# Differential attention's scores on all 128 rows of TensorE: stacked queries, doubled keys, key rests beside zeros

## The reference, cut to what matters

```python
q = (h @ w_q).reshape(b, nb, Q_BLOCK, N_HEADS, 2, HEAD_DIM)        # HEAD_DIM = 64
logits = einsum('bqhmd,bkhmd->bhmqk', q, k) * HEAD_DIM ** -0.5     # m: the two maps
logits = where(dist >= 0, logits + bias, -inf)
probs = softmax(logits)
attn = probs[:, :, 0] - lam * probs[:, :, 1]
o = einsum('bhqk,bkhe->bqhe', attn, v)
```

## Time and profile before

| | us |
|---|---|
| median of 3 runs | 1964.98 (1963.58 to 1965.52) |
| span of the profiled execution | 1962.9 |
| PE busy, share of the span | 1940.2, 99% |
| DVE, ACT, POOL busy | 1248.2, 827.2, 319.8 |
| granted TensorE clock, mean | 0.997 |

### The profile page before, as it was taken

How to read it: one execution, slowest core, us unless ns; L and a number is a source line. 1 busy time by engine, 2 the same in 40 slices (tenths; PEclk the granted TensorE clock), 3 DMA queues, 4 the chain that set the end, 5 groups by cost and what they waited for, 6 DMA issues and landing times.

```text
span 1962.9 us, 27288 instructions
## 1 busy us (share of the span) xinstructions
PE 1940.2 (99%) x10578; PEld 1675.1 (85%) x10578; DVE 1248.2 (64%) x2219; ACT 827.2 (42%) x1377; POOL 319.8 (16%) x257
## 2 busy tenths in 40 slices
PE   9999999999999999999999999999999999999997
PEld 8998888888888988898888889887888888888897
DVE  7676666267775754388777525786673877774256
ACT  5233333244565532344444334465554444442343
POOL 2332332101241100201111010120112011110102
PEclk9999999999999999999999999999999999999998
DMA  5323222222212235322232322232112222233221
GB/s 173 104 76 100 87 81 91 92 86 94 69 44 76 78 99 137 108 90 93 86 107 98 119 88 84 83 122 78 44 55 86 87 86 96 98 109 117 96 66 64
DMA packets 54839, 179.02 MB, mean 91 GB/s; under 512 B 6167, under 2 KB 10775, under 8 KB 54712
## 3 DMA queue, kind: packets, MB, share of 16 engines
q1 hardware_dynamic: 54712, 177.29, 28.8%
HBM read 172.55 MB, written 4.72 MB: 90 GB/s over the span
## 4 chain that ended last, share of the span: by engine, by line
PE 93%; DVE 4%; ACT 1%; issue 1%; POOL 0%; DMA 0%; SPq 0%; DVEq 0%; ACTq 0%; POOLq 0%
PE pb L829 88%; PE pb L2737 1%; PE pb L932 1%; DVE WL L810 1%; PE pb L916 1%; DVE FR L1048 0%; PE pb L1767 0%; PE pb L2782 0%; DVE X L1013 0%; PE pb L920 0%; PE pb L1414 0%; DVE FR L903 0%; ACT WH L799 0%; DVE FD L1004 0%; DVE T L3011 0%
## 5 line engine op out<-in xcount | busy, mean ns | idle before, releaser
L829 PE MATMUL pb<-FR,WH 128*128 128x512 f32 (+1 forms) x5100 | 1443.2, 369 | 6.2 <-DVE FR L1048 3.2
L829 PEld LDWEIGHTS pb<-FR,WH 128*128 128x128 f32 x5100 | 914.5, 189 | 163.5 <-issue 5.9
L829 PE MATMUL pb<-FR,WL 128*128 128x512 f32 (+1 forms) x2550 | 934.9, 367 | 0.0
L810 DVE TENSOR_TENSOR WL<-stage,WH 128x1024 fp32r<-128x1024 f32 (+1 forms) x311 | 401.5, 1308 | 403.2 <-ACT WH L799 402.1
L829 PEld LDWEIGHTS pb<-FR,WL 128*128 128x128 f32 x2550 | 480.7, 189 | 79.6
L799 ACT ACTIVATE WH<-stage 128x1024 fp32r<-128x1024 f32 (+1 forms) x311 | 319.8, 1051 | 115.1 <-PE pb L829 108.6
L829 PE MATMUL pb<-WH,FR 128*128 128x256 f32 x832 | 155.9, 285 | 0.4 <-DVE WL L810 0.4
L829 PEld LDWEIGHTS pb<-WH,FR 128*128 128x128 f32 x832 | 131.6, 192 | 1.2 <-DVE WL L810 0.8
L1291 POOL TENSOR_TENSOR acc<-acc,T 128x512 f32<-128x512 f32 (+1 forms) x52 | 64.1, 1233 | 408.8 <-ACT T L1262 273.9
L829 PEld LDWEIGHTS pb<-FR 128*128 128x128 f32 x752 | 109.3, 190 | 10.8 <-issue 2.6
L829 PE MATMUL pb<-WL,FR 128*128 128x256 f32 x416 | 117.7, 283 | 0.0
(11 more groups left out here) (237 smaller groups left out, 1654.2 us busy)
## 6 DMA issues: line engine op xcount, KB each, us to landing
stage<-in_ws SPq DMA_DIRECT2D x310, 512.0 KB, 3.6
scr<-FD SPq DMA_DIRECT2D x16, 160.0 KB
X<-in_xT SPq DMA_DIRECT2D x8, 256.0 KB, 6.4
FD<-in_decay SPq DMA_DIRECT2D x8, 256.0 KB, 3.9
FD<-scr SPq DMA_DIRECT2D x1, 2048.0 KB, 8.5
out_dram<-X SPq DMA_DIRECT2D x16, 128.0 KB, 1.7
FD<-in_rope_b SPq DMA_DIRECT2D x2, 512.0 KB, 3.6
FD<-in_pT SPq DMA_DIRECT2D x4, 256.0 KB, 4.9
```

The lines of the kernel that those rows point to most:

```text
L810: dve.tensor_tensor(lo, src, hi.bitcast(F32), ALU.subtract).then_inc(*self.tick("w_lo", ("w_lo", u)))
L829: m = pe.matmul(out, l, r, start=first and i == 0, stop=last and i == n - 1)
```

## The change

A head's queries take 1024 columns as before, but now 512 columns for each map, on all 128 partitions: hi of the map on its own 64 partitions and the rest on the other 64. The keys' buffer grows from 1024 to 2048 columns: for each map, hi of the keys on both halves (512 columns), and the rest of the keys on the map's own half with zeros on the other half (512 columns). One matmul of 128 rows of stacked queries against doubled keys gives hi*hi and lo*hi in one, and a second against rest-and-zeros gives hi*lo. So a block of scores has four matmuls of 128 rows in place of six of 64.

```diff
-        self.dif_k = [fr(D0 + 4096 + 1024 * i, 1024) for i in range(2)]
+        self.dif_k = [fr(o, 2048) for o in (D0 + 4096, D0 + 10240)]
...
+    def dif_half(self, p):
+
+        return slice(64 * p, 64 * p + 64), slice(64 - 64 * p, 128 - 64 * p)
+
+    def dif_q(self, h, p):
+        return self.dif_qz[:, 1024 * h + 512 * p:1024 * h + 512 * p + 512]
...
         def scores(h, i):                                   # PE
-                for w in (("q_lo", h), ("dif_k", h)):
+                for w in (("q_lo", h), ("k_lo", h), ("k_twice", h)):
...
-            for a, b in ((0, 0), (0, 1), (1, 0)):
-                for p in range(2):
-                    hs, o = slice(64 * p, 64 * p + 64), 1024 * h + 512 * a + 128 * i
-                    m = pe.matmul(self.place["dif", "s", h, i, p][:, 0:n], QZ[hs, o:o + 128],
-                                  K[hs, 512 * b:512 * b + n], start=(a, b) == (0, 0), stop=a == 1)
-                    if a == 1:
-                        m.then_inc(*self.tick("pe_scores", ("pe", "dif", "s", h, i, p)))
+                o = 1024 * h + 512 * p + 128 * i
+                q, both, rest = QZ[:, o:o + 128], K[:, 512 * p:512 * p + n], K[:, 1024 + 512 * p:1024 + 512 * p + n]
+                self.mm(pe, self.place["dif", "s", h, i, p][:, 0:n], [(q, rest), (q, both)]).then_inc(
+                    *self.tick("pe_scores", ("pe", "dif", "s", h, i, p)))
...
         def query(h):                                       # ACT
-            act.activation(QZ[:, 1024 * h:1024 * h + 512], self.place["t", "dif", "q", h], ACT.Copy).then_inc(
-                *self.tick("q_hi", ("q_hi", h)))
+            for p in range(2):
+                rows = slice(0, P) if p == 0 and h >= 4 else self.dif_half(p)[0]
+                act.activation(self.dif_q(h, p)[rows, :], t[rows, :], ACT.Copy).then_inc(
+                    *self.tick("q_hi", ("q_hi", h, p)))
+
+        def query_rest(h):                                  # ACT, heads 4 to 7
+            act.wait_ge(*self.at("q_rest", h))
+            for p in range(2):
+                own, other = self.dif_half(p)
+                act.activation(self.dif_q(h, p)[other, :], self.place[t][own, :], ACT.Copy)
...
         def key(h):                                         # ACT
-            if h >= 3:
-                rounded(h - 3)
             if h % 2 == 0:
                 self.hi_to(act, BLOCK["w_kv_2", KD - 1, h])
-                if h:
-                    self.hi_to(act, BLOCK["w_kv_2", 3, 9 + h])
...
-            act.activation(self.dif_k[h % 2][:, 0:512], self.place["t", "dif", "k", h], ACT.Copy).then_inc(
-                *self.tick("k_hi", ("k_hi", h)))
+            for p in range(2):
+                own, _ = self.dif_half(p)
+                act.activation(K[own, 512 * p:512 * p + 512], self.place["t", "dif", "k", h][own, :],
+                               ACT.Copy).then_inc(*self.tick("k_hi", ("k_hi", h, p)))
+            if h and h % 2 == 0:
+                self.hi_to(act, BLOCK["w_kv_2", 3, 9 + h])
+            if h >= 3:
+                rounded(h - 3)
+            act.wait_ge(*self.at("k_hi", h, 1))
+            for p in range(2):
+                own, other = self.dif_half(p)
+                k = K[:, 512 * p:512 * p + 512]
+                act.activation(k[other, :], k[own, :].bitcast(F32), ACT.Copy).then_inc(
+                    *self.tick("k_twice", ("k_twice", h)))
...
-        for h in range(6):                                  # ACT's order
+        for h in range(2):
             query(h)
         self.hi_to(act, BLOCK["w_q_2", KD - 1, 7])
+        for h in range(2, 5):
+            query(h)
         query(6)
         query(7)
         key(0)
         self.hi_to(act, BLOCK["w_kv_2", KD - 1, 9])
+        query(5)
         value(0, [0])
...
             if h < 7:
                 scores(h, 1)
+                if h == 0:
+                    query_rest(4)
+                    query_rest(5)
...
             turn(h, 1)
             if h < 7:
                 c = (h + 1) // 2
+                if h == 0:
+                    query_rest(6)
+                    query_rest(7)
                 value(c, [(h + 1) % 2])
...
+        def query_rest(h):                                  # DVE, heads 0 to 3
+            dve.wait_ge(*self.at("q_hi", h, 1))
+            for p in range(2):
+                own, other = self.dif_half(p)
+                q = self.dif_q(h, p)
+                dve.tensor_tensor(q[other, :], self.place[t][own, :], q[own, :].bitcast(F32), ALU.subtract)
...
         def key(h):                                         # DVE
-            if h % 2 == 0:
+            if h == 0:
                 self.lo_to(dve, BLOCK["w_kv_2", KD - 1, h])
...
+            if h and h % 2 == 0:                            # behind the scaling, L2992
+                self.lo_to(dve, BLOCK["w_kv_2", KD - 1, h])
...
         for h in range(6):                                  # DVE's order
             query(h)
+        query_rest(0)
         self.lo_to(dve, BLOCK["w_q_2", KD - 1, 7])
         query(6)
         query(7)
+        query_rest(1)
         key(0)
+        query_rest(2)
         self.lo_to(dve, BLOCK["w_kv_2", KD - 1, 9])
+        query_rest(3)
         value(0, [0])
...
         def key(h):                                         # POOL
-            pool.wait_ge(*self.at("k_hi", h))
-            pool.tensor_tensor(o[:, 512:1024], self.place[t], o[:, 0:512].bitcast(F32), ALU.subtract)
+            for p in range(2):
+                own, _ = self.dif_half(p)
+                pool.wait_ge(*self.at("k_hi", h, p))
+                if p:
+                    pool.wait_ge(*self.at("k_lo first", h))
+                pool.tensor_tensor(K[own, 1024 + 512 * p:1536 + 512 * p], self.place[t][own, :],
+                                   K[own, 512 * p:512 * p + 512].bitcast(F32), ALU.subtract)
+            pool.wait_ge(*self.at("k_lo", h))
...
+        def zeros(h, after):
+            pool.memset(self.dif_k[h][:, 1024:2048].bitcast(F32), 0.0)
...
+        zeros(0, ("pe", "ffn0", "o", 7))                    # POOL's order
+        query(4)
+        zeros(1, ("pe", "dif", "q", 7))
+        query(6)
+        query(7)
         key(0)
+        query(5)
```

More of the change, by code:

```diff
@@ L2851, in query @@
         def query(h):
+            t = self.place["t", "dif", "q", h]
             act.wait_ge(*self.at("q_in", h))
-            act.activation(QZ[:, 1024 * h:1024 * h + 512], self.place["t", "dif", "q", h], ACT.Copy).then_inc(
-                *self.tick("q_hi", ("q_hi", h)))
+            for p in range(2):
[3 more added lines that the diff above has]
+        def query_rest(h):
+            t = ("t", "dif", "q", h)
+            act.wait_ge(*self.at("q_rest", h))
+            for p in range(2):
+                own, other = self.dif_half(p)
+                act.activation(self.dif_q(h, p)[other, :], self.place[t][own, :], ACT.Copy).then_inc(
+                    *self.tick("q_shifted", ("q_lo", h), ("free", *t)))
         def key(h):
-            if h >= 3:
-                rounded(h - 3)
+            K = self.dif_k[h % 2]
             if h % 2 == 0:
                 self.hi_to(act, BLOCK["w_kv_2", KD - 1, h])
-                if h:
-                    self.hi_to(act, BLOCK["w_kv_2", 3, 9 + h])
             act.wait_ge(*self.at("dif_kin", h))
@@ L2983, in query @@
                 *self.tick("q_in", ("q_in", h), ("free", *b)))
+        def query_rest(h):
+            t = ("t", "dif", "q", h)
+            dve.wait_ge(*self.at("q_hi", h, 1))
+            for p in range(2):
+                own, other = self.dif_half(p)
+                q = self.dif_q(h, p)
+                dve.tensor_tensor(q[other, :], self.place[t][own, :], q[own, :].bitcast(F32), ALU.subtract).then_inc(
+                    *self.tick("q_rest", ("q_lo", h), ("free", *t)))
         def key(h):
-            if h % 2 == 0:
+            if h == 0:
                 self.lo_to(dve, BLOCK["w_kv_2", KD - 1, h])
@@ L3159, in key @@
         def key(h):
-            t, o = ("t", "dif", "k", h), self.dif_k[h % 2]
-            pool.wait_ge(*self.at("k_hi", h))
-            pool.tensor_tensor(o[:, 512:1024], self.place[t], o[:, 0:512].bitcast(F32), ALU.subtract).then_inc(
-                *self.tick("k_lo", ("dif_k", h), ("free", *t)))
+            t, K = ("t", "dif", "k", h), self.dif_k[h % 2]
+            if h < 2:
+                pool.wait_ge(*self.at("k_zeros", h))
+            for p in range(2):
[4 more added lines that the diff above has]
+                pool.tensor_tensor(K[own, 1024 + 512 * p:1536 + 512 * p], self.place[t][own, :],
+                                   K[own, 512 * p:512 * p + 512].bitcast(F32), ALU.subtract).then_inc(
+                    *self.tick("k_lo", *([("k_lo", h), ("free", *t)] if p else [("k_lo first", h)])))
+            pool.wait_ge(*self.at("k_lo", h))
+        def zeros(h, after):
+            pool.wait_ge(*self.at(*after))
```

(15 more changed lines are left out.)

## The result

| | before | after |
|---|---|---|
| time, median | 1964.88 us (1963.58 to 1966.81, 6 runs) | 1972.16 us (1970.68 to 1974.0, 6 runs) |
| ratio to before | | 1.0037, interval 1.0027 to 1.0047 |
| span of the profiled execution | 1962.9 us | 1970.3 us |

The change costs 7.3 us, 0.37%. The forecast was 3.0 us slower, and 1972.16 lies just above its range, 1960.5 to 1972.

A forecast was written before the change was run, and what follows sets the result against it. PE, busy 99% of the span, was taken as the bound, with ACT and DVE pacing odd heads. Terms -2.7 + 2.4 + 2.3 + 1.0 = +3.0 us gave 1968.0 us on the median; range 1960.5 to 1972.

The forecast's parts named there:

- PE's saving kept: Cheaper score blocks on PE, kept only in blocks 1 to 3 of heads 0, 2, 4 and 6: -2.7 us.
- POOL's hold in heads 3 and 5: POOL's key-rest subtractions delay DVE's L3031 ahead of the combine by 1.2 us in each head: +2.4 us.
- the entry, first bias: Before the first values, extra ACT copies and DVE query rests make the first bias late: +2.3 us.
- ACT's chain in head 0: Four ACT copies for query_rest(6) and (7) ahead of head 0's values make these late into head 1: +1.0 us.
- PE's blocks: Four full matmuls a block: 0.91 us from block 3's start to the next matmul, PE saving 0.87 us a head.
- PE to wait at scores(4,1): At scores(4,1), start of head 4, PE's wait was to grow from 0.42 us to nearly 2 us.
- The clearing: POOL's clearing of 1024 columns in front of query(6): from nothing to 2.6 us, taken as 1.3 us.
- Rival D: Entry jams as rests alternate with POOL: +4 us, 1.5 more for a clearing; +6 to +7, so 1971.5; chance 0.14.
- rival A: The forecast itself, summed over entry and heads: +3.0 us, from +0.5 to +5.5 by the bounds; chance 0.50.
- Rival E: Full score blocks on PE aren't cheaper, 0.65 us more a head: +8 us, 1973; chance 0.04.

The follow-up runs named there:

- experiment 1: Kernel before with only PE's scores changed to four 128-row matmuls a block over the old buffers, output not the reference's: 1963.9 us, 0.9994.
- experiment 2: Changed kernel with ACT's rounded copy of an older head put back ahead of the key, as before the change: 1968.47 us, 1.0019.
- experiment 3: Changed kernel with DVE's query rests 2 and 3 moved from the entry to behind the biases of scores(0,1) and scores(0,2): 1970.87 us, 1.003.
- experiment 9: experiment 6 with ACT's two doubling copies of key 1 in head 0 moved behind the exponentials of scores(0,3): 1964.74 us, 0.9998.
- experiment 4: Changed kernel with matmuls nobody reads filling PE's waits ahead of scores(0,1), turn(3,2) and turn(5,2): 1968.99 us, 1.0022.
- experiment 5: Changed kernel with the moves of experiment 2 and experiment 3 together: 1966.42 us, 1.0006.
- experiment 6: experiment 5 with the rest of query 7 made by DVE in head 0, ahead of its values, instead of by POOL and ACT: 1966.2 us, 1.0004.
- experiment 11: Changed kernel with all its ACT, DVE and POOL work, but three pairs of 64-row matmuls for each block of scores: 1973.93 us, 1.0049.

## Why the prediction missed

The forecast was +3.0 us, and the profiled execution after is 7.26 us late. By its own terms:

| term | forecast | measured | from |
|---|---|---|---|
| PE's saving kept | -2.7 | -1.70 alone; -2.45 as the remainder | experiment 1; 7.53 less the four lines below |
| POOL's hold in heads 3 and 5 | +2.4 | +1.95 | after against experiment 2 |
| the entry, first bias | +2.3 | +3.70 | after; experiment 3 |
| ACT's chain in head 0 | +1.0 | +1.07 | (0,3) to (1,0); experiment 9 |
| TensorE's low clock behind the waits | none | +3.26 | after against experiment 4 |
| behind the stage | none | -0.27 | 7.53 at its end, 7.26 at the end of the span |

- **PE's blocks cost what was forecast** (0.91 us for scores(0,3)), and the saving is kept in even heads only. Its amount there was put too high: 0.67 us for a head, and 0.4 to 0.5 came through in experiment 1. I had counted block 1, which in heads 2, 4 and 6 stands behind a wait and saves next to nothing. The remainder of the sum gives 2.45, but this number carries the errors of all other lines; in experiment 5, where no hold and no low clock is left, it is 1.80 (1.08 less 1.82 and 1.06).
- **POOL and DVE meet in heads 3 and 5** as forecast, and experiment 2 shows that it is the place of one copy on ACT that makes them meet. The Trainium skill ("SBUF — State Buffer", Who interferes with whom) says that a DVE instruction with two SBUF inputs contends with a GpSimd instruction that reads SBUF; L3075 at 1.70 us beside POOL's subtraction and at 0.62 without it agrees. I had expected PE to wait at scores(4,1). The wait came earlier, 1.67 us ahead of turn(3,2), as L3075 feeds these transposes.
- **The entry was mis-sized.** I put it at 2.3, between 0.9 without exclusion and 4 with it. It is 3.7. Four of DVE's query rests took 5.15 us (2.77 + 2.38) where they take 2.8 undisturbed, and experiment 3, which moves just these, gives 1.88 back. The clearing that I had priced at 1.3 us takes 0.95, while DVE was idle; the two weight rests ahead of the values weren't held (2.43 us, 2.36 in experiment 3). Rival D had the entry's size (+4) about right, and the reason only in part: POOL held the query rests, not these weight rests. That D's 1971.5 is the nearest of all the rivals' times is luck: its 1.5 us for a clearing aren't there, and the low clock isn't in it.
- **ACT's chain in head 0** came out at the size that was forecast, 1.07 for 1.0. I had put it down to the four query rests ahead of the values; experiment 9 shows that the doubling copies ahead of the exponentials are part of it, as moving them alone takes 1.09 us off in experiment 6.
- **The step that failed is that a wait of PE was priced at its own length.** My sum, and each rival, has PE at the rate of the rows before the change, so that the low clock stands in it at nothing, and no row was looked at for it. Behind waits of 2.73, 1.67 and 1.71 us the granted clock is 0.5 for 3.41 us, and this has cost 3.3 of the 4.3 us by which I missed; the entry's 1.4 more and POOL's 0.45 less are most of the rest. The wait itself was in the forecast (I wrote that waits of nearly 2 us would come in heads 4 and 6); what stands behind one was not. Without the low clock the loss is 4.0 us by the traces (7.26 - 3.26) and 4.1 by the medians (1968.99 in experiment 4), inside the +0.5 to +5.5 of rival A.
- **A sum that was wrong.** Rival E added the price of dearer blocks, 5.2 us, to the forecast's +3.0, which still holds the saving of 2.7. By its own terms it is 5.2 + 2.4 + 2.3 + 1.0 = +10.9, so 1976, and not 1973. It had a chance of 0.04, and the blocks of 0.91 us rule it out.
- **What stays open.** Experiment 4 shows what the low clock costs and that it goes when PE's idle time is filled; it doesn't show what decides. In the stage the waits of 1.67 to 3.03 us all have it behind them (after, experiments 2, 3 and 11), and those of 0.77 us (head 3 of experiment 2), 0.88 (experiment 3), 1.41 and 1.35 (heads 3 and 5 of experiment 11) don't. Elsewhere the length doesn't decide it: before, a wait of 1.41 us at the kernel's end has the low clock 0.8 us behind it (1951.55), and at 1270.60 in experiment 4 it comes behind waits of 0.50 and 0.35 us.

## What to carry to other kernels

Where one engine is busy 99% of the time, ask what it does behind each new wait, and not only how long it waits: here three waits of 6.1 us together brought slow matmuls that cost 3.3 us more, and useless matmuls put into them made the kernel faster. A saving on the busiest engine that is paid for on the others has to be weighed at the places where those others set the pace, and the first of them is the entry of a stage, where all of them begin late. When an order is written by hand, move the added instructions one by one: one copy's place was worth 3.7 us, and five such moves (one of them to another engine) took the kernel from 7.3 us slower to no difference that these runs can tell, with nearly the same work to do.

## What was unexpected in the hardware

- Behind PE's waits of 2.73, 1.67 and 1.71 us, in a stretch where PE is otherwise nearly always busy, the granted clock was 0.5 for 3.41 us each; a pair of matmuls of 512 columns took 1.05 us there and 0.62 outside. The same work with the same short waits ran at 1.00 in one execution and had such a stretch at 1270.60 in another (experiment 4).
- A copy on ACT or a subtraction on DVE or POOL over 64 partitions takes as long as over 128: ACT's 16 copies of queries, of both sizes, take 613 to 633 ns each, on DVE one half of a rest took 0.69 us and a scaling of 128 x 512 took 0.68, and on POOL a key's rest over 64 partitions took 1.29 us at the median, as over 128 before (1.30). So a key's copy, split by halves of the partitions, took 1.29 us (two of L2880) where the whole one took 0.63 (L2866).
- POOL's clearing of 128 x 1024 took 0.95 us, less than its subtraction over half as many columns (1.30 us), over the same 128 partitions.
